# Forgetting attention: mask additions and rounding on GpSimd, the output copy on VectorE, one copy of turned blocks

## The reference

```python
def forgetting_attention(h, w_q, w_o, k, v, F):
    b, s, _ = h.shape
    q = (h @ w_q).reshape(b, s, B_HEADS, HEAD_DIM)      # 16 heads of 64
    ...
        causal = q_pos[:, None] >= k_pos[None, :]
        decay = jnp.transpose(Fqb, (0, 2, 1))[..., None] - F_k[:, :, None, :]
        logits = jnp.einsum('bqhd,bkhd->bhqk', qb, k).astype(jnp.float32) * scale + decay
        logits = jnp.where(causal, logits, -jnp.inf)
        p = jax.nn.softmax(logits, axis=-1)
        return jnp.einsum('bhqk,bkhd->bqhd', p.astype(v.dtype), v)
    ...
    return o.reshape(b, s, B_WIDTH) @ w_o
```

## Time and profile before

| | us |
|---|---|
| median of 3 runs | 2129.16 |
| lowest and highest | 2129.04, 2130.63 |
| the profiled execution | 2130.89 |
| its span (first to last instruction) | 2128.9 |
| PE busy | 1791.4 (84%) |
| PE weight loads | 1506.0 (71%) |
| DVE busy | 1734.3 (81%) |
| ACT busy | 861.6 (40%) |
| POOL busy | 543.4 (26%) |

### The profile page before, as it was taken

How to read it: one execution, slowest core, us unless ns; L and a number is a source line. 1 busy time by engine, 2 the same in 40 slices (tenths; PEclk the granted TensorE clock), 3 DMA queues, 4 the chain that set the end, 5 groups by cost and what they waited for, 6 DMA issues and landing times.

```text
span 2128.9 us, 30905 instructions
## 1 busy us (share of the span) xinstructions
PE 1791.4 (84%) x11460; PEld 1506.0 (71%) x11460; DVE 1734.3 (81%) x3010; ACT 861.6 (40%) x1352; POOL 543.4 (26%) x474
## 2 busy tenths in 40 slices
PE   5999898999999998999999999999666655554655
PEld 4998798999999987899899999989222222221221
DVE  5887777878977888754689998748999989998877
ACT  3444566544554446644545445554212112111101
POOL 0110002111001110211320002422555554455441
PEclk7999999999999998999999999999877688778678
DMA  7889733688767894254545444527999999999996
GB/s 318 318 318 372 295 127 146 256 310 297 288 258 300 295 328 165 100 198 165 175 175 198 164 176 170 184 100 301 409 422 422 422 422 422 422 423 422 422 422 263
DMA packets 88783, 606.25 MB, mean 285 GB/s; under 512 B 9763, under 2 KB 11059, under 8 KB 21468
## 3 DMA queue, kind: packets, MB, share of 16 engines
q1 hardware_dynamic: 37708, 245.03, 31.8%
q0 software_dynamic: 37040, 270.57, 30.6%
q10 hardware_dynamic: 13920, 89.15, 10.4%
HBM read 601.53 MB, written 3.18 MB: 284 GB/s over the span
## 4 chain that ended last, share of the span: by engine, by line
PE 22%; DVE 18%; DMA 15%; issue 3%; ACT 2%; POOL 1%; DVEq 0%; POOLq 0%; ACTq 0%
DMA row_pair<-in_peer_uv,mod_ring 15%; PE ps L821 12%; DVE row_pair L2580 4%; DVE w_lo L1909 3%; DVE XTOK L2599 3%; PE ps L1317 2%; PE ps L852 2%; DVE work L2350 2%; PE ps L953 2%; DVE SQ L2350 2%; PE ps L954 1%; POOL row_pair L793 1%; PE ps L884 1%; PE ps L1027 0%; ACT w_hi L1339 0%
## 5 line engine op out<-in xcount | busy, mean ns | idle before, releaser
L1909 DVE TENSOR_TENSOR w_lo<-raw,w_hi 128x2048 fp32r<-128x2048 f32 (+1 forms) x248 | 526.9, 2127 | 192.1 <-ACT w_hi L1339 191.4
L1317 PE MATMUL ps<-row_pair,diag 128*128 128x512 f32 x512 | 358.2, 865 | 264.1 <-ACT diag L1876 264.1
L1339 ACT ACTIVATE w_hi<-raw 128x2048 fp32r<-128x2048 f32 (+1 forms) x248 | 440.2, 1776 | 219.5 <-PE ps L821 70.3
L1317 PEld LDWEIGHTS ps<-row_pair,diag 128*128 128x128 f32 x512 | 137.0, 281 | 484.7 <-ACT diag L1876 319.4
L821 PE MATMUL ps<-HH,w_hi 128*128 128x256 f32 x1584 | 447.8, 283 | 0.4 <-DVE w_lo L1909 0.3
L821 PE MATMUL ps<-HL,w_hi 128*128 128x256 f32 x1584 | 444.5, 281 | 0.0
L821 PE MATMUL ps<-HH,w_lo 128*128 128x256 f32 x1584 | 443.3, 280 | 0.0
L793 POOL DMA_INDIRECT row_pair<-in_peer_uv,mod_ring x256 | 326.8, 1276 | 325.3 <-PE ps L1317 219.1
L2580 DVE SCALAR_TENSOR_TENSOR row_pair<-row_pair,HTOK 128x1024 f32<-128x1024 f32 x256 | 312.1, 1220 | 62.0 <-DMA row_pair<-in_peer_uv,mod_ring 59.6
L821 PEld LDWEIGHTS ps<-HL,w_hi 128*128 128x128 f32 x1584 | 298.3, 188 | 0.7 <-issue 0.7
L821 PEld LDWEIGHTS ps<-HH,w_lo 128*128 128x128 f32 x1584 | 298.4, 188 | 0.0
(11 more groups left out here) (336 smaller groups left out, 3007.3 us busy)
## 6 DMA issues: line engine op xcount, KB each, us to landing
raw<-in_f_in SPq DMA_DIRECT2D x88, 1024.0 KB, 4.8
mod_ring<-in_ada ACTq DMA_DIRECT2D x74, 1024.0 KB, 7.1
raw<-in_f_out SPq DMA_DIRECT2D x64, 704.0 KB, 5.7
raw<-in_mix_a SPq DMA_DIRECT2D x16, 1024.0 KB, 4.8
raw<-in_mix_g SPq DMA_DIRECT2D x8, 1024.0 KB, 4.9
raw<-in_pq SPq DMA_DIRECT2D x8, 1024.0 KB, 5.1
first<-in_ada ACTq DMA_DIRECT2D x4, 1024.0 KB, 12.9
raw<-in_a_q SPq DMA_DIRECT2D x4, 1024.0 KB, 5.2
```

Of the source, the lines that this page charges most:

```text
L1317: last = mm(ps[:, 2 * t + c, :], diag[:, d, :], row_v(k)[:, c * 512:(c + 1) * 512], start=False, stop=False)
L1339: f(slot(w_hi, g), slot(raw, g), ACT.Copy).then_inc(hi_ready, 1)
L1909: v.tensor_tensor(slot(w_lo, g), slot(raw, g), f32(slot(w_hi, g)), ALU.subtract).then_inc(low["v"], 1)
```

## The change

The mask is added by GpSimd for all eight steps at once, as soon as the decay lines have landed; for that the masked lines of the first 128 queries get a place for each head. GpSimd also computes the low halves of keys 3 to 7, and both halves of each output. VectorE copies the output of step s-2 from PSUM, between `logits` of s+1 and `probs` of s, and the last two at the end. ScalarE keeps the exponentials and copies both banks of turned blocks in one instruction, for which the banks of the stage are dealt out anew (scores in 4, 5 and 2, 3, turned blocks in 6 and 7).

```diff
-        decay0 = mod_ring[:, 0:2 * P].rearrange("p (a n) -> p a n", a=2)
+        decay0 = mod_ring[:, 0:B_HEADS * P].rearrange("p (a n) -> p a n", a=B_HEADS)
...
+        TURN_BANK = {"B": (6, 7), "X": PT_BANK}
+        ps_b = (ps[:, 4:6, :], ps[:, 2:4, :])
...
@@ gpsimd
-            lows("attB", OT)
+            pool.wait_ge(decay_loaded, 16)
+            pool.wait_ge(mods_ready, summed(ADA_TILES // 2 - 1))
+            causal = mask[:, P:SEQ].unsqueeze(1).broadcast_to([P, 2, P])
+            for c in range(DC):
+                keys = decay[:, 2 * c:2 * c + 2, :]
+                nc.gpsimd.tensor_tensor(decay0[:, 2 * c:2 * c + 2, :], keys[:, :, 0:P], causal, ALU.add)
+                nc.gpsimd.tensor_tensor(keys[:, :, P:SEQ], keys[:, :, P:SEQ], causal, ALU.add).then_inc(decay_masked, 1)
+            pool.wait_ge(kl_ready, 3)
+            for c in range(3, DC):
+                pool.wait_ge(kh_ready, c + 1)
+                nc.gpsimd.tensor_tensor(KL[:, c, :], KS[:, c, :], f32(KH[:, c, :]), ALU.subtract).then_inc(kl_ready, 1)
+            for c in range(DC):
+                pool.wait_ge(attn_ready, STEP0["B"] + c + 1)
+                nc.gpsimd.tensor_copy(HH[:, c, :], OT[:, c, :]).then_inc(hh_ready, 1)
+                pool.wait_ge(hh_ready, SET["attB"] + c + 1)
+                nc.gpsimd.tensor_tensor(HL[:, c, :], OT[:, c, :], f32(HH[:, c, :]), ALU.subtract).then_inc(hl_ready, 1)
...
@@ scalar, attention
-                        f(OT[:, c, :], ps[:, 0, 0:SEQ], ACT.Copy).then_inc(attn_ready, 1)
...
-                        f(HH[:, c, :], OT[:, c, :], ACT.Copy).then_inc(hh_ready, 1)
...
+                    if kind == "B":
+                        f(PT[s % 2][:, :, 0:n], ps[:, TURN_BANK["B"][0]:TURN_BANK["B"][1] + 1, 0:n], ACT.Copy).then_inc(probsT_ready, 1)
+                        return
...
                     turned_copy(s)
-                    if s > s0:
-                        output(s - 1)
-                output(s1 - 1)
...
@@ vector, logits
-                    dve.wait_ge(logits_ready, 2 * s)
-                    step(v.tensor_tensor(decay0, keys[:, :, 0:P], causal, ALU.add), lag=1)
-                    step(v.tensor_tensor(keys[:, :, P:SEQ], keys[:, :, P:SEQ], causal, ALU.add))
+                    dve.wait_ge(decay_masked, c + 1)
...
@@ vector, attention
+                def low(s):
+
+                    dve.wait_ge(pv_done, s + 1)
+                    v.tensor_copy(OT[:, s - s0, :], ps[:, 0, 0:SEQ]).then_inc(attn_ready, 1)
+
...
                         logits(s + 1)
-                    if kind == "B" and s - s0 + 3 < DC:
-                        key_low(s - s0 + 3)
+                    if kind == "B" and s > s0 + 1:
+                        low(s - 2)
                     probs(s)
+                if kind == "B":
+                    low(s1 - 2)
+                    low(s1 - 1)
```

More of the change, by code:

```diff
@@ L486, in build_program @@
         decay_loaded = sem("decay_loaded")
+        decay_masked = sem("decay_masked")
         mem_loaded = sem("mem_loaded")
@@ L998, in scores @@
                         for m in range(2):
-                            o = ps_s[qt][:, m, 0:nk]
+                            o = ps_b[qt][:, m, 0:nk]
                             r = slice(64 * m, 64 * m + 64)
@@ L1010, in turn_probs @@
                     for m in range(2):
-                        bank = PT_BANK[m]
+                        bank = TURN_BANK[kind][m]
                         blocks = [(0, 0), (0, 1), (1, 1)] if kind != "X" else [(0, 0), (0, 1), (1, 0), (1, 1)]
@@ L1615, in output @@
                     act.wait_ge(pv_done, s + 1)
[L1616 to L1619, removed]
-                        f(OT[:, c, :], ps[:, 0, 0:SEQ], ACT.Copy).then_inc(attn_ready, 1)
-                    act.wait_ge(attn_ready, s + 1)
[L1622 to L1625, removed]
-                        f(HH[:, c, :], OT[:, c, :], ACT.Copy).then_inc(hh_ready, 1)
+                    f(OT[:, 4 * c:4 * c + 4, :].rearrange("p (a b) n -> p a (b n)", a=2), ps[:, 0:2, :],
+                      ACT.Copy).then_inc(attn_ready, 1)
+                    act.wait_ge(attn_ready, s + 1)
+                    for k in range(4 * c, 4 * c + 4):
+                        f(EH[:, k, :], OT[:, k, :], ACT.Copy).then_inc(eh_ready, 1)
                 def turned_copy(s):
@@ L2106, in logits @@
                 if kind == "B":
-                    causal = mask[:, P:SEQ].unsqueeze(1).broadcast_to([P, 2, P])
-                    keys = decay[:, 2 * c:2 * c + 2, :]
-                    dve.wait_ge(logits_ready, 2 * s)
-                    step(v.tensor_tensor(decay0, keys[:, :, 0:P], causal, ALU.add), lag=1)
-                    step(v.tensor_tensor(keys[:, :, P:SEQ], keys[:, :, P:SEQ], causal, ALU.add))
+                    dve.wait_ge(decay_masked, c + 1)
                 for qt in range(TT):
@@ L2126, in logits @@
                         else:
-                            src, b = ps_s[qt][:, m, 0:nk], decay[:, 2 * c + m, :] if qt else decay0[:, m, :]
+                            src, b = ps_b[qt][:, m, 0:nk], decay[:, 2 * c + m, :] if qt else decay0[:, 2 * c + m, :]
                         last = v.tensor_tensor_reduce(out=LG[:, qt, m, 0:nk], in0=src, in1=b,
@@ L2304, in _ @@
                 key_low(c)
-            dve.wait_ge(decay_loaded, 16)
             attention("B")
```

## The result

The changed kernel takes 2136.66 us (median of 8 runs, 2134.86 to 2137.61) against 2129.18 beside it: a ratio of 1.0031, 95% interval 1.0021 to 1.0040, slower by 4.5 to 8.5 us. The forecast was 2127.6, with 2124.9 to 2133.0 as its range and 0.10 for slower. The profiled execution took 2137.61 us, its span 2135.8.

The account below looks back on a forecast made before the run. The forgetting attention was taken as a loop of waits with no full engine. Start -1.1 and steps -1.9 gave -3.0 at high clock, -0.2 with low; the middle, -1.6 from 2129.16, gave 2127.6 us, range 2124.9 to 2133.0.

Parts of the forecast that it names:

- the low clock at the middle that I took: Attention loop: PE's low clock where it was costs +2.8 us, sum -0.2; high clock gives -3.0; -1.6 taken between.
- to the first reciprocal: Start of the attention: first scores added 0.79 earlier, so VectorE's first reciprocal comes at 833.91 instead of 835.0, -1.1 us.
- seven intervals: Attention steps between VectorE's eight reciprocals: 23.9 us against 25.8 at the high clock, -1.9; two low-clock steps would add 2.8.
- The masks are hidden: Ahead of the attention: sixteen GpSimd mask additions done by about 826.5, 4 us to spare, at no cost.
- The round trip: Each step with an output copy: VectorE's products, PE's turn and values, copy and reciprocal follow one another, 3.35 us.
- The wait in every step: VectorE idle ahead of each output copy until PE's values: 0.5 to 0.7 us at high clock, 2 at low.
- The cast: GpSimd's cast behind each output copy collides with VectorE's products: 0.25 us per step, making the period 3.6.
- the port: Attention steps: GpSimd and VectorE collide when reading SBUF; only the cast was charged, 0.25 us per step.
- a rival with a chance of 0.10: Cast and subtraction both land on VectorE's products: 1.06 us per step rather than 0.25, total +3.3, 2132.5; chance 0.10.
- the signs that I had listed: Expected in the next profile, among others: products of 1.2 to 1.6 us, reciprocals 3.3 to 3.9 apart at high clock.
- the end: no change: Last output copies up to the projection: VectorE's copies at the same places, 0.42 against 0.38 long, GpSimd's last work covered; 0.
- My rival on the clock: PE stays at its low clock through the loop, 1.38 us more per step: +5.3, 2134.5; chance 0.10.

Follow-up runs that it names:

- second traces: The changed kernel and the kernel before, unedited, each traced once more: 2134.57 us and 2130.12 us, one run each.
- the runs at 3.56 and 3.37: Changed kernel with GpSimd's subtraction held until VectorE's products are done, 2125.84 us; changed kernel with only the cast moved to ScalarE, 2126.12 us.

## Why the prediction was wrong

By the stage's own terms, forecast and trace, the low clock at the middle that I took:

| term | forecast | trace |
|---|---|---|
| to the first reciprocal | -1.1 | -0.9 (4.81 to 3.94 from the first scores) |
| seven intervals | -0.5 | +2.5 (25.71 to 28.22) |
| last reciprocal to projection | 0 | +2.1 (5.67 to 7.74) |
| projection | 0 | +1.5 (35.59 to 37.07) |
| sum | -1.6 | +5.2 |

*Right, and shown.* The masks are hidden, though with 1.5 us to spare and not 4: the first addition started 3 us later than I put it, behind the decay lines (their DMA was issued at 802.89 in this trace, not at 800.1), and three of them took 2.8 each behind VectorE's weight splits. The round trip was put at 3.35 and is 3.37 when nothing hinders the products. The wait in every step is 0.69, where I wrote 0.5 to 0.7. The cast was put at 0.25 and costs 0.20; with it alone the step is 3.56, where I wrote 3.6. That size was partly luck: I scaled it by how long the instructions last, and what counts is how much of one is left when the product starts (last section). The single copy takes 0.81, forecast 0.78.

*The step that failed first: "the port".* I charged the cast alone and left the subtraction to a rival with a chance of 0.10, on the ground that it waits for the cast and VectorE has by then gone on to the scores. It starts 0.42 behind the start of products that last 1.03, so it always meets the second. Its price stood in my own row, 0.53, and that is what it measured; six steps of 0.5 are the 3.0 us by which the intervals miss. That rival had the mechanism, its 1.06 was too much: the two together are 0.72. Two of the signs that I had listed showed it at once: products of 1.75 where I wrote 1.2 to 1.6, reciprocals 4.09 apart where I wrote 3.3 to 3.9.

*The step that failed second: "the end: no change".* The copies do stand at the same places, and at the high clock the tail is 4.9 to 5.7 us in the experiments. But I let the low clock lie only where the trace of before had its first fall. Inside the loop that was nearly right (4.56 and 5.03 against 4.09 make +1.4, the middle that I took). What I didn't ask is what the slower step does to PE: it waits 1.52 us per step for products, and the clock falls a second time, later and longer than before (13.7 us against 6.8), over the tail and 3.4 us of the projection. With PE kept busy, 4.4 of the 5.2 us are gone. My rival on the clock thought only of the steps of the loop.

The two failures are one chain: with the subtraction held, or the cast elsewhere, the clock holds and the stage is 6.7 or 6.5 us shorter, where the products alone give back 3.2 or 4.3 in six steps. What makes the clock fall again in one loop and not in another isn't settled by these runs. The pace alone doesn't say: the runs at 3.56 and 3.37 had no second fall, in one trace each, and the kernel before had one in both traces, in the first behind steps of 3.92 and 3.59.

*Open.* The medians differ by 7.5 us and the stage by 5.2 (5.8 in the second traces). The interval includes both; the traces show no place for the rest. The same holds for the experiments: against the changed kernel their medians fell by 0.3 to 4.2 us more than their stages, except with the masks on VectorE, where the one trace has the longer stage. Outside the stage the traced executions of all kernels differ by 7 us.

## What to carry to other kernels

When work moves to an engine that shares something with the engine it left, follow the whole chain that its trigger starts, the second instruction too, and lay its start times beside the neighbour's. An instruction that waits costs by its place in the queue: the same copy one place further back waits for nothing, moves its followers beside harmless work, and turns a loss of 0.3% into a gain of 0.4%. In a loop of waits, a step that grows by a few tenths can also cost PE its clock, and a part of that bill came in the next stage here.

## What the runs showed of the hardware

VectorE's products, with both inputs in SBUF, lose less than the GpSimd instruction beside them lasts: 0.20 to a cast of 0.40, 0.53 to a subtraction of 0.78. What counts is how much of that instruction is left when the product starts. In the step shown the first product starts 0.35 ahead of the cast's end and takes 0.62 instead of 0.42; the second starts 0.66 ahead of the subtraction's end (at 851.16, which is 852.37 less its 1.21; the subtraction ends at 851.82) and takes 1.21 instead of 0.68. Each loses what is left less 0.13 to 0.15, and the other five steps are alike. Score lines, with one input in PSUM, lost nothing to either (0.28 beside a cast of 0.40), and moving both there took the whole 0.72 away. The Trainium skill, SBUF — State Buffer, Who interferes with whom, says that only VectorE instructions with two inputs in SBUF, or in a mode that takes both ports, contend, and that they block for the whole instruction; the first agrees with these rows. By the second, the products would lose the 0.35 and 0.66 that are left when they start; they lost 0.20 and 0.53.

PE's clock fell after stretches in which PE was far from idle: busy for 11.98 of 20.48 us ahead of the second fall, in waits of 1.52 us a step and a last one of 2.41, and in the kernel before for 9.82 of 13.65. Matmuls without any use, put where PE waited, kept it at 2.4 GHz and took 4.4 us out of the trace.
